# A range mask added in sixteen pieces, memory tiles spread over four units, and two weight splits moved ahead of a gate

## The reference, cut to what matters

```python
for layer in range(2):                                  # first block
    x = x + mixer(rms_norm(x, mix_norm))                # layer 0: window and MLA; layer 1: dilated attention
    x = x + memory_cross_attention(rms_norm(x, x_norm), rms_norm(mem, mem_norm), w_q, w_kv, w_o)
    x = x + (silu(h @ w_gate) * (h @ w_up)) @ w_down    # h = rms_norm(x, ffn_norm), hidden width 2816
for l in range(2):                                      # second block, with a context stream in layer 0
    p, u, vs, q, k, v, gl = split(modulate(rms_norm(h)) @ w_in[l])
    s_win = q . k_win * scale + rpb[dr, dc]             # neighbourhood of 8 rows x 16 columns, 8 heads
    attn = softmax([s_win, q . k_ctx]) @ [v_win, v_ctx]
    h = h + g1 * ((sum of three sigmoid-gated branches) @ w_o)
    h = h + g2 * square(relu(modulate(rms_norm(h)) @ w_ff1)) @ w_ff2
return rms_norm(h)
```

## Time and profile before

| | us |
|---|---|
| median of 3 runs | 2135.91 (2134.17 to 2136.14) |
| the profiled execution | 2134.76 |
| its span, first to last instruction | 2132.9 |
| PE busy | 2023.6 (95%) |
| DVE busy | 1155.0 (54%) |
| ACT busy | 887.9 (42%) |
| POOL busy | 164.6 (8%) |
| mean granted clock of TensorE | 0.973 |

### The profile page before, as it was taken

The page is one execution under the profiler, slowest core; times in us unless marked ns, Lnnn a source line. Parts: engine busy times, 40 slices in busy tenths (PEclk is TensorE's granted clock), DMA queues, the critical chain, the costliest instruction groups (busy, mean ns, idle before and its releaser), DMA issues.

```text
span 2132.9 us, 35259 instructions
## 1 busy us (share of the span) xinstructions
PE 2023.6 (95%) x14824; PEld 1795.6 (84%) x14824; DVE 1155.0 (54%) x1975; ACT 887.9 (42%) x1483; POOL 164.6 (8%) x165
## 2 busy tenths in 40 slices
PE   7799899999988999999999999999999798999998
PEld 7769899998787999878678877777777687999997
DVE  6655566577456666524534445444444634666664
ACT  4555544444554444414522334222222425455442
POOL 0030100001122000002600000000000003000000
PEclk9899999999999999989999999999999999999999
DMA  7255499845654655413533324445444330664553
GB/s 224 82 192 159 130 218 237 216 158 157 220 161 118 194 179 166 140 42 125 157 87 96 108 80 154 162 145 171 138 158 139 128 91 29 176 198 142 187 186 100
DMA packets 331163, 317.16 MB, mean 149 GB/s; under 512 B 16997, under 2 KB 315756, under 8 KB 330750
## 3 DMA queue, kind: packets, MB, share of 16 engines
q1 hardware_dynamic: 324160, 297.84, 45.8%
q0 software_dynamic: 3904, 12.03, 2.9%
q10 hardware_dynamic: 2942, 5.04, 0.7%
HBM read 306.01 MB, written 8.85 MB: 148 GB/s over the span
## 4 chain that ended last, share of the span: by engine, by line
PE 86%; DVE 6%; DMA 3%; ACT 3%; issue 1%; POOL 0%; ACTq 0%; SPq 0%; DVEq 0%; POOLq 0%
PE acc L663 24%; PE acc L664 23%; PE acc L665 23%; DVE w_low L1792 3%; DMA raw<-in_l_w_up 2%; PE pss L828 2%; PE pst L839 2%; PE acc L678 1%; PE acc L680 1%; PE acc L679 1%; ACT w_high L1306 1%; PE acc L751 1%; PE acc L854 1%; PE pso L854 1%; PE acc L811 1%
## 5 line engine op out<-in xcount | busy, mean ns | idle before, releaser
L1792 DVE TENSOR_TENSOR w_low<-raw,w_high 128x1024 fp32r<-128x1024 f32 (+4 forms) x503 | 571.3, 1176 | 176.6 <-ACT w_high L1306 175.8
L663 PE MATMUL acc<-normed,w_high 128*128 128x256 f32 (+2 forms) x2008 | 639.1, 318 | 15.1 <-DVE w_low L1792 14.9
L1306 ACT ACTIVATE w_high<-raw 128x1024 fp32r<-128x1024 f32 (+4 forms) x503 | 471.6, 984 | 412.1 <-PE acc L665 385.0
L664 PE MATMUL acc<-normed,w_high 128*128 128x256 f32 (+2 forms) x2008 | 633.3, 315 | 0.0
L665 PE MATMUL acc<-normed,w_low 128*128 128x256 f32 (+2 forms) x2008 | 632.8, 315 | 0.0
L663 PEld LDWEIGHTS acc<-normed,w_high 128*128 128x128 f32 (+1 forms) x2008 | 387.0, 193 | 45.2 <-DVE w_low L1792 17.4
L665 PEld LDWEIGHTS acc<-normed,w_low 128*128 128x128 f32 (+1 forms) x2008 | 386.7, 193 | 22.9
L664 PEld LDWEIGHTS acc<-normed,w_high 128*128 128x128 f32 (+1 forms) x2008 | 387.0, 193 | 22.1
L663 PE MATMUL acc<-inner,w_high 128*128 128x256 f32 (+2 forms) x1232 | 387.7, 315 | 2.6 <-DVE inner L1805 2.4
L664 PE MATMUL acc<-inner,w_high 128*128 128x256 f32 (+2 forms) x1232 | 385.6, 313 | 0.0
L665 PE MATMUL acc<-inner,w_low 128*128 128x256 f32 (+2 forms) x1232 | 385.1, 313 | 0.0
(11 more groups left out here) (227 smaller groups left out, 2132.3 us busy)
## 6 DMA issues: line engine op xcount, KB each, us to landing
raw<-in_w_ff SPq DMA_DIRECT2D x128, 512.0 KB, 4.3
raw<-in_w_mod SPq DMA_DIRECT2D x96, 512.0 KB, 4.7
raw<-in_w_in SPq DMA_DIRECT2D x84, 512.0 KB, 4.1
raw<-in_l_w_gate SPq DMA_DIRECT2D x44, 512.0 KB, 4.9
raw<-in_l_w_up SPq DMA_DIRECT2D x44, 512.0 KB, 4.6
raw<-in_l_w_down SPq DMA_DIRECT2D x32, 512.0 KB, 4.6
raw<-in_l_w_qkv SPq DMA_DIRECT2D x24, 512.0 KB, 4.6
raw<-in_l_w_out SPq DMA_DIRECT2D x16, 512.0 KB, 4.5
```

The lines of the kernel that those rows point to most:

```text
L663: mm(dst, lh, rh, start=i == 0, stop=False)
L664: mm(dst, lh, rl, start=False, stop=False)
L1306: nc.scalar.activation(WH[:, s % NSPLIT, w0:w0 + nw], RAW[:, r:r + nw], ACT.Copy)\
L1792: V.tensor_tensor(WL[:, s % NSPLIT, c], RAW[:, r:r + nw], WH[:, s % NSPLIT, c].bitcast(F32), ALU.subtract).then_inc(w_low, 1)
```

## The change

The mask is added row by row: sixteen POOL instructions of 128x256 per table, each behind a wait for the low part of one further unit. `bias_split` holds the first unit that is waited for: for the first table the one behind the first of layer 1's feed-forward, for the second the one behind the next of the branches after the first neighbourhood attention. DVE's wait now asks for 16 counts per table. `memory(1)` is called for one tile at a time, behind the rope of steps 2 to 5 of layer 1's q and k units, and ACT does three splits, then four times one high and one split, then one split. In the feed-forward of the first block the split that stood behind the subtraction of the first pair now stands ahead of it: on ACT in front of SiLU, on DVE right behind the scaling of the gate.

```diff
--- before.py
+++ after.py
@@ -555,7 +555,7 @@
         out_sem = sem("out_sem")
         split_free = {}
         rotated = {}
-        ffn_split = []
+        ffn_split, bias_split = [], []
         raw_free = {}
         pair_bank, cols_bank = {}, {}
 
@@ -1036,6 +1036,8 @@
                 ready = one_by_one()
                 done = {}
                 ffn_split.append(st["split"])
+                if l:
+                    bias_split.append(st["split"] + 1)
                 for kind, c in ffn_turns:
                     tiles = FFN_CHUNKS[c][1]
                     if kind == "in" and c == 0:
@@ -1141,6 +1143,8 @@
 
                 attention(na_tasks(l), 0 if l else MODS, lead=lambda: values(1, blocks=[0, 1, 2, 3]), tail=gate_tail,
                           keys=st["acc"] - 3, ropes=st["rope"] - 1)
+                if l == 0:
+                    bias_split.append(st["split"] + 1)
                 need(st["store"] - (8 if l == 0 else 4))
                 pe.wait_ge(cols_free, st["pair"])
                 for src, kt in ((pot(T), 2), (sot(T), 2), (ot_na(T), 4)):
@@ -1251,9 +1255,10 @@
                         pool.dma_start(dst, src).then_inc(bias_in, 16)
                 pool.wait_ge(bias_in, 16 * 16 * (l + 1))
                 win = const("window")
-                every = bass.AP(tensor=win.tensor, offset=win.offset, ap=[list(win.ap[0]), [0, NB * NA_H], [1, S]])
-                flat = view(BIAS, 0, (NB * NA_H, S))
-                nc.gpsimd.tensor_tensor(flat, flat, every, ALU.add).then_inc(bias_done, 1)
+                for i in range(NB * NA_H):
+                    pool.wait_ge(w_low, split_pieces[bias_split[l] + i])
+                    row = BIAS[:, i // NA_H, i % NA_H, :]
+                    nc.gpsimd.tensor_tensor(row, row, win, ALU.add).then_inc(bias_done, 1)
 
             rope(swa_raw, cos64, "swa")
             attention(swa_tasks + mla_tasks, lead=lambda: rope(mla_raw, cos_mla, "mla"))
@@ -1546,9 +1551,11 @@
                     st["acc"] += 1
                     split()
                     root(KD, S)
-                    split()
-                    highs(mem_chunks())
-                    split(7)
+                    split(3)
+                    for i in range(4):
+                        highs(mem_chunks()[i:i + 1])
+                        split()
+                    split()
                     st["acc"] += 13
                     act.wait_ge(acc_free[g % 4], g // 4 + 1)
 
@@ -1606,7 +1614,8 @@
                             g = st["acc"]
                             st["acc"] += 1
                             highs([hidden(c, S).tiles(m, m + 2)], ready=(acc_free[g % 4], g // 4 + 1))
-                            split()
+                            if m or c:
+                                split()
                     elif (kind, c) == ffn_turns[-1]:
                         act.wait_ge(gain_done, 3)
                         if l:
@@ -2134,7 +2143,6 @@
                     rooted_row(column=True)
                     dve.wait_ge(skew_w, 16 * 18)
                     times_row(dil_raw[0], g, 64 ** -0.5)
-                    memory(1)
                     for i in range(1, 10):
                         if i < 8:
                             times_row(dil_raw[i], st["acc"], 64 ** -0.5 if i < 4 else 1.0)
@@ -2142,6 +2150,8 @@
                         split()
                         if i > 1:
                             rope(dil_raw[i - 2:i - 1], sin64)
+                        if 2 <= i < 6:
+                            memory(1, i - 2, i - 1)
                     attention(dil_tasks, MODS)
                     st["acc"] += 2
                 for m in banks(8, S):
@@ -2174,10 +2184,8 @@
                                 inverted(S)
                                 split()
                                 rooted_row()
-                                times_row(gate, g)
-                            else:
-                                times_row(gate, g)
-                                split()
+                            times_row(gate, g)
+                            split()
                             dve.wait_ge(gated, st["sig"])
                             link(V.tensor_tensor(gate, gate, RROW2, ALU.mult))
                             b, free = bank()
@@ -2269,7 +2278,7 @@
                     if i:
                         rope(na_raw(T)[i - 1:i], sin_axial)
                 st["acc"] += 2
-                dve.wait_ge(bias_done, l + 1)
+                dve.wait_ge(bias_done, NB * NA_H * (l + 1))
                 attention(na_tasks(l), 0 if l else MODS)
                 mod_gain(l, 1)
                 for b3 in range(3):
```

## The result

The median of four runs is 2109.4 us (2106.42 to 2110.28), beside 2136.02 us (2134.17 to 2137.57) for four runs of the kernel before: a ratio of 0.9873, 95% interval 0.9856 to 0.989. The change took 26.6 us off. The prediction was 2108.6 us. The profiled execution took 2109.75 us, with a span of 2108.0.

The account below looks back on a forecast made before the run. PE, busy 95%, gains only where it waits for w_low splits that DVE delivers late. 10.51 + 7.86 + 5.85 + 1.56 + 1.56 = 27.3 us off 2134.8 gives 2107.4, plus 1.15 for the median: 2108.6 us; 8-in-10 range 2103 to 2118.

Parts of the forecast that it names:

- Part 1, the holes: Range mask's long POOL adds hold DVE at layer 1's feed-forward entry and block two's branches; removing them gains 10.51 and 7.86 us.
- Part 1, the pieces: Sixteen short mask adds per table, about 0.8 us each on POOL, cost PE 0.
- the upper end: Most the mask pieces could cost PE: 2.4 us, eight second splits with 0.3 us exposed each.
- Part 2: Layer 1's q and k units: one memory tile per unit removes a 6.25 us loss, 0.4 comes back; gain 5.85 us.
- the slack of 3.2: Tile units: w_low ends 4.4 us after a unit's end, PE takes it up at 7.65; DVE lateness that can be borne.
- rival A: DVE bounds the four tile units, late passes all exposed; 5.85 shrinks to about 1.6, 2113 us; chance 0.12.
- Part 3: Both layers' feed-forward: split ahead of the first gate's products removes PE's 1.56 us wait, twice; layer 0 bounds 0 to 1.56.
- B: Pieces hit second splits (2.4), layer 0's feed-forward takes back 1.56, tile passes late too: 2117 us; chance 0.10.
- C: DVE stalls at 646.8 and 1059.5 are not POOL's doing, or pieces come in a bunch: 2127 us; chance 0.04.
- D: Slower: every piece takes the port ahead of a DVE instruction PE waits for, 41.9 us against 27.3: 2150.5 us; chance 0.03.

Follow-up runs that it names:

- all tiles at once: Changed kernel with all four memory tiles at one place again, but two units later, behind the rope of step 2: 2107.48 us.
- light traffic: Changed kernel with layer 0's skew writes cut to an eighth: 2102.6 us; the same with the first pair's split behind the subtraction again: 2106.17 us.
- after again: The changed kernel, unaltered, run once more beside the second set of kernels: 2105.61 us.

## Why the prediction was right, point by point

**Part 1, the holes.** 10.51 and 7.86 us were predicted. Undone alone, the part loses 10.0 to 10.6 and 7.87 us. Taking a stretch of layer 0 as the twin of layer 1 gave the whole price, where the idle time alone (8.61 and 4.68) would have given 13.3 of 18.4. In the changed kernel the gained subtractions take 0.88 us again (DVE's timeline), and the sigmoids come every 6.80 us (ACT's, to be compared with the earlier trace rows):

```profile
643.01 0.88 DVE L1912 SCALAR_TENSOR_TENSOR normed<-resid,vec,normed 128x256 fp32r<-128x256 f32 x2 [1.75 <-ACT normed L1363]
```

```profile
1047.86 0.60 ACT L1715 ACTIVATE scores<-acc 128x512 f32<-128x512 f32 x1 [4.07 <-PE acc L665]
1054.66 0.60 ACT L1715 ACTIVATE scores<-acc 128x512 f32<-128x512 f32 x1 [4.07 <-PE acc L665]
```

**Part 1, the pieces.** I estimated 0.8 us a piece; the group of POOL has 32 of 0.865 us in the mean, and POOL's timeline shows 0.74 alone, 1.12 behind a DVE instruction and 1.81 for the first of the second table:

```profile
L1261 POOL TENSOR_TENSOR bias<-bias,cst 128x256 f32<-128x256 f32 x32 | 27.7, 865 | 173.3 <-DVE w_low L1801 170.8 <-DMA bias<-skew 2.5
```

```profile
663.61 1.12 POOL L1261 TENSOR_TENSOR bias<-bias,cst 128x256 f32<-128x256 f32 x1 [5.82 <-DVE w_low L1801]
...
676.51 0.74 POOL L1261 TENSOR_TENSOR bias<-bias,cst 128x256 f32<-128x256 f32 x1 [5.93 <-DVE w_low L1801]
...
1043.53 1.81 POOL L1261 TENSOR_TENSOR bias<-bias,cst 128x256 f32<-128x256 f32 x1 [2.46 <-DMA bias<-skew]
```

The 1.81 is over the 1.3 that I had given as the most, and costs nothing. PE sees 0 of them, as taken; the 2.4 us of the upper end did not come even at four times the work.

**Part 2.** The wait went and the rotations are 6.62 us apart: 6.25 us, as predicted. Then I let DVE fall behind by 0.86 to 1.19 us per tile unit, 3.4 to 4.8 in all, and took 0.4 us back; none came back. DVE's timeline shows what a pass with a tile costs:

```profile
461.46 0.69 DVE L1926 SCALAR_TENSOR_TENSOR work<-acc,scores 128x512 f32<-128x512 f32 x1 [1.73 <-PE acc L665]
...
469.25 0.68 DVE L1926 SCALAR_TENSOR_TENSOR work<-acc,scores 128x512 f32<-128x512 f32 x1
469.85 2.86 DVE L1801 TENSOR_TENSOR w_low<-raw,w_high 128x1024 fp32r<-128x1024 f32 x2
...
476.07 0.68 DVE L1926 SCALAR_TENSOR_TENSOR work<-acc,scores 128x512 f32<-128x512 f32 x1
...
482.89 0.68 DVE L1926 SCALAR_TENSOR_TENSOR work<-acc,scores 128x512 f32<-128x512 f32 x1
...
490.69 0.68 DVE L1926 SCALAR_TENSOR_TENSOR work<-acc,scores 128x512 f32<-128x512 f32 x1
```

The first pass, to 469.25, takes 7.79 us, the 7.81 of the prediction. To 476.07 and on to 482.89 it is 6.82 us each time; the last, to 490.69, is 7.80, since there a subtraction (L1814, 1.68 us for 0.69) is held by the rope product. Behind the first none waits for PE, as I had said. The over-sized term is the split in the two middle passes: I took a pass from the earlier trace rows, where w_low takes 3.40 us and is preceded by a 0.33 us wait, and 3.40 was itself a w_low held by POOL's rope product, which begins 0.12 us ahead of it. POOL's timeline, before and then after:

```profile
479.08 1.30 POOL L1228 TENSOR_TENSOR work<-work,rope 128x512 f32<-128x512 f32 x1 [5.32 <-PE acc L811]
```

```profile
469.06 1.43 POOL L1232 TENSOR_TENSOR work<-work,rope 128x512 f32<-128x512 f32 x1 [5.38 <-PE acc L811]
```

That product follows PE's rotation, not DVE. A DVE that is late comes to its w_low 0.79 us after the product began, is held for 0.5 us in place of 1.0 (2.86 against 2.36 undisturbed), and needs no wait for w_high. The pace is 6.62, so the four passes add 1.17, 0.20, 0.20 and 1.18 us: DVE is at most some 2.75 us late, within the slack of 3.2 that I had worked out. In the kernel with all tiles at once the pass takes 12.0 us (458.87 to 470.86), so DVE is 5.4 us late, not the 4.5 that I expected of it: 0.9 is the held tile product shown above. By the slack of 3.2 PE would have waited 2.2 us, and it waited 0.93, because the slack has the same over-sized split in it: there the late DVE begins w_low 0.6 us into its pass and takes 2.35 us, so w_low ends 3.0 us behind the pass's start and not 4.4, and the slack is some 4.7 (an estimate), which leaves 0.7 us to wait. Slack and lateness were the right two numbers; the prediction had both wrong in size, one too small and the other too large, and rival A failed by that.

**Part 3.** 1.56 us in each layer; measured 1.8 in layer 1, the hole and 0.2 around it that no row accounts for (the granted clock is 1.00 from 681 to 685 us in the kernel before). In layer 0 the compared profiles differ by 0.8 us, but the split by itself gives 1.8 with light traffic, and 192.24 against 194.67 with full traffic is 2.4. The range of 0 to 1.56 was too narrow on the upper side. New waits for late loads, which I had put at none, did come in the compared profile (0.35 and 0.78 us, where before had 0.36 and 0.47), and took about 1 us of the part's worth there; five of the profiles with the early split have none that cost anything. ACT's SiLU table load moved behind the new split, and the scaling it serves still ends ahead of DVE's split (ACT's timeline, then DVE's: SiLU is done at 663.2, w_low at 663.5):

```profile
661.30 1.28 ACT L1612 ACT_TABLE_LOAD   x1
662.59 0.63 ACT L1612 ACTIVATE scores<-scores 128x512 f32<-128x512 f32 x1
```

```profile
660.57 0.69 DVE L1926 SCALAR_TENSOR_TENSOR scores<-acc,scores 128x512 f32<-128x512 f32 x1
661.18 2.35 DVE L1801 TENSOR_TENSOR w_low<-raw,w_high 128x1024 fp32r<-128x1024 f32 x2
```

**The sum.** The terms as measured are 10.0 to 10.6, 7.87, 5.4 to 6.25, 1.8, and 0.8 to 2.4, together 25.9 to 28.9 us, against 27.3 predicted; the medians differ by 26.6 in the first comparison and by 29.4 for after again. That the first hit the forecast to 0.8 us is in part luck, since code that no edit touches moves by more than that between profiles.

**The rivals.** A: no wait came back at the seventh unit. B: of its three terms one was seen in part, the late loads in layer 0. C: both stalls came back with the long add, and in neither of the other two kernels with a part undone. D: 128 adds cost nothing.

## What to carry to other kernels

A long instruction on one engine can hold short ones on another for its whole length; cut it, and let each piece follow an event after which the other engine has slack: cutting gave 12.8 of 18.4 us here, the pace 5.6. Price a hole by a stretch without it (a twin layer, the steady pace), not by its idle time, which was 13.3 of 18.4 us here. When chunks of side work stand ahead of what the bounding engine waits for, first move them to where the buffers are full, then ask whether to spread them: the first was worth 4 to 5 us, the second 1.2; and before taking a duration from a row as the price of a later pass, see whether the row was itself held by something.

## What the runs showed of the hardware that I had not expected

**The port between POOL and DVE changes hands after each instruction, even under a full queue.** Sixteen adds in a row took 17.52 us, 1.10 each where one alone takes 0.74, and w_low pairs beside them 3.42 us where 2.36 is normal. The products with one operand in PSUM (L1991) stayed at 0.67 to 0.69. The Trainium skill ("SBUF — State Buffer", "Who interferes with whom") has the lock going to whichever came first, for the whole of one instruction; the runs agree with that for an instruction alone. What the runs add is that a queue on one side does not keep the lock, and that is why cutting helps without any pace.

**Not only instructions with two SBUF operands were held.** The tile products of L1934 (TENSOR_SCALAR) read one 128x256 operand and a column from SBUF. The pair that stood beside the rope product took 1.53 us where 0.62 is normal.

**Untouched code moves by up to 5 us from profile to profile, and the granted clock differs with it.** Up to the mean square ahead of layer 0's cross-attention the kernels of this study took from 182.2 to 187.0 us. The windows of 4 us from the changed kernel, and then from the one with the single add (busy PE, PEld, DVE, ACT, POOL; granted clock, DMA):

```profile
24.00:28.00 4.00, 4.00 (x23) 3.94 (x23) 3.62 (x7) 2.70 (x4) 0.00 (x0) 0.63 0.82 155
```

```profile
24.00:28.00 4.00, 4.00 (x33) 4.00 (x33) 3.65 (x6) 2.53 (x3) 0.00 (x0) 0.93 0.86 159
```

PE is busy in all of it both times, but at a granted clock of 0.63 in one and 0.93 in the other (1.2 GHz for a good part of it, or 2.4 GHz for nearly all of it), and does 23 matmul records against 33. It had been partly idle in the 8 us before in both. This window is only a part of the 4.8 us between these two: at the next mean square (L779, 37.41 and 36.16 us) they are 1.25 us apart, and most of the rest comes between 80 and 187 us, where the granted clock is 0.80 against 0.90 from 80 to 110 us and 0.89 against 0.94 from 120 to 150. Why one execution gets its clock back some us earlier than another I did not find, and no run here tells it. For a change of 1 to 3 us the stretches say more than the medians.
